# Moving 32 of 384 tokens out of the first expert matmuls of a PEER layer, and reordering filler work, dots and gates

## The chip, the cores and the metric

The kernel runs on one core of a Trainium2 chip. The metric is the time of one execution on the device in microseconds. The kernel before takes 1738.43 us, the median of three runs (1738.17 to 1740.97). The engines are TensorE (PE, with its weight loads as PEld), VectorE (DVE), ScalarE (ACT), GpSimd (POOL) and SyncE (SP, which only issues DMAs here). Each runs its own instructions in order; semaphores tie them together.

## The reference

One transformer layer on 512 tokens of 1024 float32 values.

- Token mixer: one projection `x @ w_in` gives the inputs of four attention branches, four heads of 64 each (top-128 selected keys; a window of 128 with sinks; block attention; stick-breaking), and four gates of 1024 columns. `merged = sum(sigmoid(g) * (y_branch @ w_branch))`, then `merged @ w_out`, a residual and a layer norm.
- PEER feed-forward: `q = x @ wq`; for each token and each of 8 heads two sets of 128 scores, the top 16 of each, the top 16 of their sums: 128 experts per token of 16384, with softmax gates. Then

```
h   = gelu(dot(x[token], u[expert]))      # 128 experts per token
out = sum over experts of gate * h * v[expert]
```

and a residual and a second layer norm.

## The kernel before, in words

Float32 products are made of three matmuls on halves: each operand is split into a high part (`w_hi`, `tok_hi`, written by ACT as a rounded copy) and a low part (`w_lo`, `tok_lo`, the difference, written by POOL or DVE), and `three` (line 1282) adds hi x hi, hi x lo and lo x hi. Weights come as units of 128 x 1024 values, loaded by SP into one of four `raw` slots (`load_unit`, line 337), split by ACT (`split_hi`, L535) and by POOL (`split_lo`, L435, `expert_lo`, L482) or DVE (`value_lo`, L1054). The counters `hi_done`, `lo_pool`, `lo_dve` and `unit_done` tie these steps; `raw`, `w_hi` and `w_lo` slots come free in the same order.

The order of the work is written out by hand, the same on every engine:

1. Attention. The first 9 of 38 units, then 32 items (`N_ITEM`), each one pair of heads on one tile of 128 queries. In step s PE does `scores(s + 1)`, `weights(s)`, `outputs(s - 1)` and then one whole projection unit as filler (`unit_at`: none in steps 16, 20 and 31). DVE does the softmax work of the item and `choose_keys` (`CHOICES[s]` rounds of top-8 removal for the key selection). The first unit waits for the low part of x, pair of chunks by pair of chunks.
2. Merge. For each of 8 column chunks four `branch` matmul groups, into four banks; DVE multiplies each with its gate (`prod`, L959) and adds (L962 to L966). `branch(c, b)` waits on `merge_step` for the first add of an earlier chunk.
3. Output projection, first norm, transposes of the new token tiles (`transpose_h`), their high and low parts (`hT_high` on ACT, `hT_low` on DVE), the query projection and the sub-key scores.
4. Experts, the dense way for tiles 1 to 3 (384 tokens, `DT`): for each of 128 units PE computes the activations of 128 experts for all 384 tokens (`project` at L1284 to L1286, 24 matmuls), ACT applies gelu (L703) and stores it to DRAM (`gelu_d`). Beside this, DVE routes one tile after the other (`route`: top-k, positions, gates), and in a marking stretch the gates of the tile are spread to a dense 128 x 128 table per token: `mark` builds one-hot rows for four tokens (a quad), ACT or DVE scales one side (L719, L1182), PE multiplies them (`gates_of`, L1571), ACT collects them in `stage` (L728) and stores 8 quads at a time to `gate_d` (L735). 14 units per routing stretch, 16 units with 2 quads each per marking stretch, 22 units in the tail (`TAIL`).
5. Tile 0 goes another way: POOL fetches for each of its 128 tokens the row `u[expert]` by an indirect DMA (`get_u`, L491), one fetch for all 128 partitions, into one of five slots, and DVE takes the dot with x (`dot`, L1060, x lies in PSUM banks 6 and 7). 128 dots; 30 per marking stretch, 3 or 6 per routing stretch, the rest in the tail. Later POOL fetches `v[expert]` (`get_v`, L499) and DVE adds it up with weight gate x gelu (`fma`, L1072), 128 of them between value units 2 and 116.
6. Value units: for each of 128 units DVE multiplies the stored gates (`gate_in`) with the stored activations (`gelu_in`) (`times_gelu`, L1195), ACT and DVE split the product, and PE does 18 matmuls of 512 columns (L1472 to L1475). SP loads the gates of the first 16 units in two parts (L373) at the weight loads P-8 and P-4 of the expert units, the rest later.
7. Second norm and stores.

What the diff and the steps of the prediction touch: `FIRST_UNITS`, `ROUTE_UNITS`, `MARK_UNITS`, `dots_by` (lines 65 to 93), `unit_at` (137), `load_gates` (365), `get_u` (485), `scale_match` (712), `store_gates` (733), `norm` (973), `dot` (1057), `route` (1075), `mark` (1170), `project` (1288), `branch` (1399), `last_units` (1478) and the loops that call them.

Of the kernel before, what the change touches and what calls it, by code (L numbers as in the profile page):

```python
# [24 lines left out]
P = 128  # L25
# [39 lines left out]
FIRST_UNITS, ROUTE_UNITS, MARK_UNITS = 16, 14, 16  # L65
TAIL = FIRST_UNITS + 3 * (ROUTE_UNITS + MARK_UNITS)
ROUTE_DOTS, MARK_DOTS = (3, 6, 6), 30
U_SLOTS, V_SLOTS = 5, 6
FMA_START, FMA_END = 2, P - 12
# [4 lines left out]
def routed_at(j):  # L74

    return FIRST_UNITS + (j - 1) * (ROUTE_UNITS + MARK_UNITS)


def dots_before(b):

    return sum(ROUTE_DOTS[:b]) + MARK_DOTS * b


def dots_by(k):

    if k < FIRST_UNITS:
        return 0
    b, at = divmod(k - FIRST_UNITS, ROUTE_UNITS + MARK_UNITS)
    if k >= TAIL:
        return min(P, dots_before(3) + (P - dots_before(3)) * (k - TAIL + 1) // (P - TAIL - 4))  # L90
    if at < ROUTE_UNITS:
        return dots_before(b) + ROUTE_DOTS[b] * max(0, at - 6) // (ROUTE_UNITS - 7)
    return dots_before(b) + ROUTE_DOTS[b] + MARK_DOTS * (at - ROUTE_UNITS + 1) // MARK_UNITS
# [38 lines left out]
CHOICES = [3] * 8 + [1] * 8 + [3, 2, 2, 2, 2, 3, 2]  # L132
# [4 lines left out]
def unit_at(s):  # L137

    n = N_FIRST + s - (s > 16) - (s > 20)
    return None if s in (16, 20) or n >= N_ATT or s < 0 else n  # L140
# [27 lines left out]
def peer_block(nc, xT, x_rows, w_units, u_units, v_rows, u_rows, sinks, ln1_g, ln1_b, subk, ln2_g, ln2_b,  # L168
# [98 lines left out]
    def sem(name):  # L267
# [17 lines left out]
    y_hi_set, y_lo_set, sig_kept, branch_full, merge_step, m_set = (sem(n) for n in (  # L285
        "y_hi_set", "y_lo_set", "sig_kept", "branch_full", "merge_step", "m_set"))
# [14 lines left out]
        "eid_set", "dot_done", "own_gelu", "fma_done", "own_x"))  # L301
    u_in = [sem(f"u_in{i}") for i in range(U_SLOTS)]
# [6 lines left out]
    def wait_lo(engine, n):  # L309
# [22 lines left out]
    with nc.Block() as block:  # L332
# [3 lines left out]
        def _(sp):  # L336
# [45 lines left out]
            def load_gelu(m):  # L382
# [5 lines left out]
                sp.dma_start(gelu_in[m % 2][:], gelu_d[:, first:first + GELU_GROUP, :])\  # L388
# [1280 lines left out]
```

## Time and profile before

| | before |
|---|---|
| median of 3 runs | 1738.43 us |
| the profiled execution | 1741.16 us |
| its span, first to last instruction | 1739.4 us |
| granted clock of TensorE, mean | 0.988 |
| PE, PEld busy | 1694.2, 1494.3 us |
| DVE, POOL, ACT busy | 1241.9, 822.3, 770.5 us |
| DMA moved | 417.65 MB, mean 240 GB/s |

Busy times are of the whole span and say nothing of a stage; the span falls into attention (to 341 us), merge and output projection (to 516), norm, queries and sub-keys (to 590), experts (to 1206) and values. A matmul's row shows when it starts and a modelled length of 0.3 to 0.4 us that overlaps with the next one's, so the pace is read from the distances of starts. An idle time stands with what ended it.

### The profile page before, as it was taken

The numbers are of one execution on the slowest core, as the hardware profiler recorded it, in microseconds if no ns is written. First come the engines' busy times: TensorE is split into PE (matmuls) and PEld (weight loads), VectorE is DVE, ScalarE is ACT, GpSimd is POOL, SyncE is SP. The second block draws the span as 40 slices with busy tenths as digits, with TensorE's granted clock in tenths as the row PEclk, the third lists the DMA queues.
The fourth block names the chain that finished last, engine by engine and source line by source line (L and its number), as shares of the span: only waits on it lengthen the run. The fifth ranks groups of instructions, "written<-read, shape, count | busy, mean of one in ns | idle before, by whom it ended". The sixth has DMA issues, their size and how long they took to land.

```text
span 1739.4 us, 24569 instructions
## 1 busy us (share of the span) xinstructions
PE 1694.2 (97%) x9061; PEld 1494.3 (86%) x9061; DVE 1241.9 (71%) x2490; ACT 770.5 (44%) x1301; POOL 822.3 (47%) x496
## 2 busy tenths in 40 slices
PE   7899979989999999999999999999999999999997
PEld 6678857778888999999999999999888888888886
DVE  2587884453244679588888988634888888888886
ACT  4444434532223443675477367534333333333332
POOL 5232222344446367776766686786423322323312
PEclk9999989999999999999999999999999999999999
DMA  5111111224233256899799789998999999999952
GB/s 199 62 61 62 49 49 61 73 85 145 71 123 109 93 182 204 280 387 359 235 333 378 259 286 384 373 369 293 406 391 354 389 370 351 379 378 353 387 193 85
DMA packets 126359, 417.65 MB, mean 240 GB/s; under 512 B 12960, under 2 KB 32416, under 8 KB 124704
## 3 DMA queue, kind: packets, MB, share of 16 engines
q1 hardware_dynamic: 70176, 232.81, 38.1%
q0 software_dynamic: 36864, 134.23, 20.5%
q10 hardware_dynamic: 19200, 49.03, 7.2%
q8 instruction: 73, 1.20, 0.3%
q14 instruction: 46, 0.38, 0.1%
HBM read 364.91 MB, written 50.86 MB: 239 GB/s over the span
## 4 chain that ended last, share of the span: by engine, by line
PE 94%; DVE 4%; DMA 1%; ACT 1%; issue 0%; POOL 0%; ACTq 0%; SPq 0%; DVEq 0%
PE ps L1284 18%; PE ps L1285 17%; PE ps L1286 17%; PE ps L1473 11%; PE ps L1475 11%; PE ps L1472 11%; PE ps L1571 5%; PE ps L1368 1%; PE ps L1393 1%; PE ps L1376 1%; PE ps L1347 1%; DVE dist_a L839 0%; DVE small L838 0%; DVE row L892 0%; DMA u_got<-u_rows,eid 0%
## 5 line engine op out<-in xcount | busy, mean ns | idle before, releaser
L1284 PE MATMUL ps<-tok_hi,w_hi 128*128 128x384 f32 (+2 forms) x1552 | 554.6, 357 | 13.4 <-DVE tok_lo L809 9.5
L1285 PE MATMUL ps<-tok_lo,w_hi 128*128 128x384 f32 (+2 forms) x1552 | 545.7, 352 | 0.0
L1286 PE MATMUL ps<-tok_hi,w_lo 128*128 128x384 f32 (+2 forms) x1552 | 545.3, 351 | 0.0
L535 ACT ACTIVATE w_hi<-raw 128x1024 fp32r<-128x1024 f32 x334 | 353.2, 1058 | 412.6 <-PE ps L1475 297.4
L482 POOL TENSOR_TENSOR w_lo<-raw,w_hi 128x1024 fp32r<-128x1024 f32 x128 | 319.3, 2497 | 164.7 <-ACT w_hi L535 164.2
L435 POOL TENSOR_TENSOR w_lo<-raw,w_hi 128x1024 fp32r<-128x1024 f32 x80 | 194.2, 2432 | 340.5 <-ACT w_hi L535 340.3
L1284 PEld LDWEIGHTS ps<-tok_hi,w_hi 128*128 128x128 f32 x1552 | 295.4, 190 | 39.1 <-issue 14.9
L1286 PEld LDWEIGHTS ps<-tok_hi,w_lo 128*128 128x128 f32 x1552 | 295.0, 190 | 19.5
L1285 PEld LDWEIGHTS ps<-tok_lo,w_hi 128*128 128x128 f32 x1552 | 295.5, 190 | 17.8
L1472 PE MATMUL ps<-w_hi,gh_hi 128*128 128x512 f32 x768 | 298.8, 389 | 0.0
L1473 PE MATMUL ps<-w_lo,gh_hi 128*128 128x512 f32 x768 | 298.8, 389 | 0.0
L499 POOL DMA_INDIRECT v_got<-v_rows,eid x128 | 151.4, 1183 | 302.6 <-DVE own L1072 285.4
L1475 PE MATMUL ps<-w_hi,gh_lo 128*128 128x512 f32 x768 | 236.4, 389 | 0.0
L1060 DVE CUSTOM_DVE_ANT_0 u_got<-u_got,ps 128x1024 f32<-128x1024 f32 x128 | 153.5, 1218 | 89.9 <-DMA u_got<-u_rows,eid 89.6
L1054 DVE TENSOR_TENSOR w_lo<-raw,w_hi 128x1024 fp32r<-128x1024 f32 x126 | 156.4, 1241 | 74.9 <-ACT w_hi L535 74.9
L1472 PEld LDWEIGHTS ps<-w_hi,gh_hi 128*128 128x128 f32 x768 | 144.2, 188 | 30.0
L1475 PEld LDWEIGHTS ps<-w_hi,gh_lo 128*128 128x128 f32 x768 | 144.1, 188 | 29.9
L1473 PEld LDWEIGHTS ps<-w_lo,gh_hi 128*128 128x128 f32 x768 | 144.1, 188 | 29.9
L1072 DVE SCALAR_TENSOR_TENSOR own<-v_got,w_own,own 128x1024 f32<-128x1024 f32 x126 | 159.9, 1278 | 0.0
L491 POOL DMA_INDIRECT u_got<-u_rows,eid x128 | 123.4, 964 | 27.2 <-issue 18.7
L703 ACT ACTIVATE gelu_t<-ps 128x384 f32<-128x384 f32 x120 | 58.8, 490 | 174.1 <-PE ps L1286 157.6
L1571 PE MATMUL ps<-right,left 128*128 128x128 f32 x768 | 93.5, 275 | 0.5 <-ACT right L719 0.5
(202 smaller groups left out, 1841.4 us busy)
## 6 DMA issues: line engine op xcount, KB each, us to landing
raw<-u_units SPq DMA_DIRECT2D x128, 512.0 KB, 4.5
raw<-v_rows SPq DMA_DIRECT2D x128, 512.0 KB, 6.8
raw<-w_units SPq DMA_DIRECT2D x78, 512.0 KB, 3.5
gate_d<-stage ACTq DMA_DIRECT2D x12, 2048.0 KB, 11.9
gelu_d<-gelu_t ACTq DMA_DIRECT2D x120, 192.0 KB, 4.5
gelu_in<-gelu_d SPq DMA_DIRECT2D x30, 768.0 KB, 7.7
gate_in<-gate_d SPq DMA_DIRECT2D x28, 768.0 KB, 11.9
gate_in<-gate_d SPq DMA_DIRECT2D x2, 1536.0 KB, 17.5
```

The lines of the kernel that those rows point to most:

```text
L435: pool.tensor_tensor(w_lo[:, n % RAW, :], raw[:, n % RAW, :], w_hi[:, n % RAW, :].bitcast(F32), ALU.subtract).then_inc(lo_done, 1)
L482: pool.tensor_tensor(w_lo[:, n % RAW, :], raw[:, n % RAW, :], w_hi[:, n % RAW, :].bitcast(F32), ALU.subtract).then_inc(lo_pool, 1)
L535: act.activation(w_hi[:, n % RAW, :], raw[:, n % RAW, :], ACT.Copy).then_inc(hi_done, 1)
L1054: dve.tensor_tensor(w_lo[:, n % RAW, :], raw[:, n % RAW, :], w_hi[:, n % RAW, :].bitcast(F32), ALU.subtract).then_inc(lo_dve, 1)
L1072: dve.scalar_tensor_tensor(own[e % 2][:], v_got[e % V_SLOTS][:], w_own[:, e:e + 1], own[e % 2][:], ALU.mult, ALU.add).then_inc(fma_done, 1)
L1284: pe.matmul(out_, l_hi, r_hi, start=start, stop=False)
L1285: pe.matmul(out_, l_hi, r_lo, start=False, stop=False)
L1286: return pe.matmul(out_, l_lo, r_hi, start=False, stop=stop)
L1472: pe.matmul(o, l_hi[:, tile_], wh, start=start, stop=False)
L1473: pe.matmul(o, l_hi[:, tile_], wl, start=False, stop=False)
L1475: last = pe.matmul(o, l_lo[:, tile_], wh, start=False, stop=stop)
L1571: last = pe.matmul(ps[:, 2 + q % 3, t * P:(t + 1) * P], left[:, s, t, :], right[:, s, t, :], start=True, stop=True)
```

## The change

- Tokens 128 to 159 (`NEAR`, 32 tokens) leave the expert matmuls: `UT` = 352 columns instead of 384, for gelu and its store too. Their activations are made like those of tile 0, by fetched rows and dots: 32 partitions times 4 groups of 32 experts each, so 32 fetches and 32 dots. Their expert numbers and x are spread over the partitions by DMAs issued on ACT. The activations after gelu are gathered by four DMAs and multiplied into the near tokens' gates before these are spread; in `gelu_in` the near columns are set to 1.
- The near tokens' quads are marked last, behind tile 3: 24, 32 and 40 quads in marking stretches of 14, 18 and 22 units. FIRST_UNITS 14, ROUTE_UNITS 17; 9 units in the tail.
- 160 dots: 12, 13, 13 in the routing stretches, 28, 36, 44 in the marking stretches, 6 in the tail and 8 beside the first value units. Three slots for the first 12, then five. fmas run from value unit 10 to 118.
- SP waits for the last gates in front of the first value weights; the first gate load follows that wait, the second comes after two weight loads. Value tile 3 uses banks 0 and 1.
- Attention: filler goes in chunks of three matmuls (`fill_to`, `filled_by`): 4 before the first scores, 4 in step -1, then 7 of 8 chunks in every step; two rounds of `choose_keys` in each of the steps 16 to 23.
- The first unit starts with the high parts of x. `branch` waits for the product that frees its bank. `transpose_h(1)` comes one unit earlier, `hT_low(0)` before the second half of the third tile's norm, `split_hi(U_WQ)` before `hT_high(0)`.

```diff
+NEAR = TOK
+UT = DT - NEAR
+NEAR_GROUPS = P // NEAR
+DOTS = P + NEAR
+FIRST_UNITS, ROUTE_UNITS, MARK_UNITS = 14, 17, (14, 18, 22)
+TAIL = FIRST_UNITS + 3 * ROUTE_UNITS + sum(MARK_UNITS)
+ROUTE_DOTS, MARK_DOTS, TAIL_DOTS, LATE_DOTS = (12, 13, 13), (28, 36, 44), 6, 8
+NEAR_FROM, NEAR_END = 54, 54 + NEAR
+FMA_START, FMA_END = LATE_DOTS + 2, P - 10
...
+def filled_by(s):
+    return 4 if s < -1 else KC + (KC * N_FILL - KC) * (s + 1) // N_ITEM
...
             for j in range(P):
                 load_unit(U_EXP + j, u_units[j])
-                if j == P - 8:
-                    sp.wait_ge(gate_read, N_QUAD)
-                    for s in range(2):
-                        sp.wait_ge(stage_out[s], 16 * (NB // 2))
-                    load_gates(0, 0)
-                if j == P - 4:
-                    load_gates(0, 1)
+            sp.wait_ge(gate_read, N_QUAD)
+            for s in range(2):
+                sp.wait_ge(stage_out[s], 16 * (NB // 2))
+            load_gates(0, 0)
             for j in range(P):
                 load_unit(U_VAL + j, v_rows[:, (j - KEPT) % P, :])
+                if j == 1:
+                    load_gates(0, 1)
...
+            def get_u(d):
+                slot, use, before = DOT_SLOTS[d]
+                near, e = dot_row(d)
+                if before is not None:
+                    pool.wait_ge(dot_done, before + 1)
...
+                if near and e == 0:
+                    pool.wait_ge(near_eid_in, 16 * NEAR_GROUPS)
...
+            def spread_near_x():
+                act.wait_ge(pick_set, 3)
+                for g in range(NEAR_GROUPS):
+                    act.dma_start(near_x[NEAR * g:NEAR * g + NEAR, :], x_tok[0:NEAR, 1, :]).then_inc(near_x_in, 16)
+            def finish_near():
+                act.wait_ge(dot_done, NEAR_END)
+                act.activation(near_dot[:], near_dot[:], ACT.Gelu).then_inc(near_gelu, 1)
...
+            def dot(d):
+                slot, use, before = DOT_SLOTS[d]
+                near, e = dot_row(d)
+                if d == NEAR_FROM:
+                    dve.wait_ge(near_x_in, 16 * NEAR_GROUPS)
+                    take_x(near_x[:], d)
+                if d == NEAR_END:
+                    take_x(x_tok[:, 0, :], d)
...
+            def weigh_near():
+                dve.wait_ge(near_h_in, 16 * NEAR_GROUPS)
+                dve.tensor_tensor(near_gate[0:NEAR, :], near_gate[0:NEAR, :], near_h[0:NEAR, :], ALU.mult)\
+                    .then_inc(near_pick, 1)
...
-                tokens = slice(P, S) if n >= U_EXP else slice(0, S)
-                to = ps[:, bank, 0:DT] if n >= U_EXP else ps[:, bank, :]
+                tokens = slice(P + NEAR, S) if n >= U_EXP else slice(0, S)
+                to = ps[:, bank, 0:UT] if n >= U_EXP else ps[:, bank, :]
...
-                    pe.wait_ge(merge_step, 4 * c - (7 if c < NH else 3))
+                    pe.wait_ge(prod_set, 4 * (c - (2 if c < NH else 1)) + (2, 3, 1, 0).index(b) + 1)
...
+            def fill_to(count):
+                while filled[0] < count:
+                    k, c = divmod(filled[0], KC)
+                    n = N_FIRST + k
+                    if c == 0:
+                        att_ready(n)
+                        wait_lo(pe, n)
+                    cols = slice(c * P, (c + 1) * P)
+                    last = three(ps[:, n % 2, :], w_hi[:, n % RAW, cols], w_lo[:, n % RAW, cols],
+                                 tok_hi[:, c, :], tok_lo[:, c, :], c == 0, c == KC - 1)
+                    filled[0] += 1
```

## Rows read from the trace of the kernel before

**Rows 1.** The page, its first part: each engine's busy us, share, instructions.
```profile
PE 1694.2 (97%) x9061; PEld 1494.3 (86%) x9061; DVE 1241.9 (71%) x2490; ACT 770.5 (44%) x1301; POOL 822.3 (47%) x496
```

**Rows 2.** Windows: length, busy us by engine, clock, DMA share, GB/s.
```profile
70.00:340.00 270.00, 255.07 (x1448) 195.45 (x1449) 191.72 (x448) 121.68 (x243) 72.95 (x30) 0.96 0.18 58
340.00:515.00 175.00, 170.39 (x752) 140.05 (x751) 71.21 (x95) 47.91 (x53) 72.65 (x32) 0.98 0.32 109
515.00:560.00 45.00, 41.23 (x277) 38.81 (x276) 25.90 (x33) 15.92 (x20) 28.85 (x12) 0.92 0.25 82
...
1019.00:1114.00 95.00, 95.00 (x641) 95.00 (x640) 80.22 (x135) 69.74 (x160) 68.01 (x48) 1.00 0.95 356
```

**Rows 3.** Timeline and chain, PE: starts of matmuls and of quads (start, length).
```profile
639.75 0.33 PE L1284 MATMUL ps<-tok_hi,w_hi 128*128 128x384 f32 x1
...
659.85 0.33 PE L1286 MATMUL ps<-tok_hi,w_lo 128*128 128x384 f32 x1
...
548.02 0.28 PE L1284 MATMUL ps<-tok_hi,w_hi 128*128 128x256 f32 x1
...
552.10 0.28 PE L1285 MATMUL ps<-tok_lo,w_hi 128*128 128x256 f32 x1
...
727.77 1.78 PE ps L1571 x16
733.72 1.78 PE ps L1571 x16
```

**Rows 4.** Timeline of the start.
```profile
7.00 6.24 DVE L809 TENSOR_TENSOR tok_lo<-x_raw,tok_hi 128x1024 fp32r<-128x1024 f32 x4 [7.00 <-ACT tok_hi L603]
...
9.48 0.77 PE L1284 MATMUL ps<-tok_hi,w_hi 128*128 128x512 f32 x1 [9.48 <-DVE tok_lo L809]
```

**Rows 5.** Windows of 8 us in the attention stage: an early item, a hole.
```profile
132.00:140.00 8.00, 7.73 (x49) 6.17 (x48) 7.05 (x16) 3.73 (x7) 2.40 (x1) 1.00 0.29 88
...
220.00:228.00 8.00, 3.23 (x12) 2.32 (x13) 7.66 (x22) 3.20 (x13) 0.00 (x0) 0.73 0.00 0
```

**Rows 6.** Timeline of the merge and of the first norm.
```profile
355.79 2.48 DVE L959 TENSOR_TENSOR prod<-ps,gates 128x512 f32<-128x512 f32 x4
...
359.14 0.76 PE L1284 MATMUL ps<-y_hi,w_hi 128*128 128x512 f32 x1 [4.37 <-DVE prod L962]
...
522.44 2.34 DVE L1006 TENSOR_TENSOR tok_lo<-ps,tok_hi 128x1024 fp32r<-128x1024 f32 x2
```

**Rows 7.** Waits: who waited for whom, us in total, times, longest.
```profile
DVE g_sum L1156 <- ACT pick L740: 20.9, 4, 10.4
...
DVE g_T L1168 <- PE ps L1560: 15.8, 3, 5.3
```

**Rows 8.** Groups of instructions by form, with count, busy us and mean ns.
```profile
L1060 DVE CUSTOM_DVE_ANT_0 u_got<-u_got,ps 128x1024 f32<-128x1024 f32 x128 | 153.5, 1218 | 89.9 <-DMA u_got<-u_rows,eid 89.6
```

**Rows 9.** A saturated window; the row fetches of the third marking stretch.
```profile
1236.00:1242.00 6.00, 6.00 (x28) 4.95 (x27) 6.00 (x9) 2.00 (x3) 4.70 (x3) 1.00 1.03 410
...
L491 POOL DMA_INDIRECT u_got<-u_rows,eid x31: 937/950/956, 1020.1 to 1113.9; - x31
...
DMA to landing us min/median/max: 5.2/8.1/12.6
```

**Rows 10.** Lines of DMAs in the tail: last gate store, gate loads, weight loads.
```profile
L735 ACTq DMA_DIRECT2D gate_d<-stage x1: 327/327/327, 1120.5 to 1120.5; - x1
...
DMA to landing us min/median/max: 10.0/10.0/10.0
...
L373 SPq DMA_DIRECT2D gate_in<-gate_d x2: 430/444/459, 1149.2 to 1165.8; - x2
...
DMA to landing us min/median/max: 17.0/17.5/18.1
...
L341 SPq DMA_DIRECT2D raw<-u_units x8: 327/363/3445, 1148.8 to 1179.4; - x8
...
DMA to landing us min/median/max: 6.2/11.8/15.2
```

More of the change, by code:

```diff
@@ new lines, in first_quad, with tile_quad, quads_of, stretch_dots @@
+def first_quad(b):
+    return max(0, 32 * (b - 1) - NEAR // 4) if b < NT else N_QUAD
+def tile_quad(q):
+    r = q + NEAR // 4
+    return r // 32 + 1, r % 32
+def quads_of(b, k):
+    first, count = first_quad(b), first_quad(b + 1) - first_quad(b)
+    return range(first + count * k // MARK_UNITS[b - 1], first + count * (k + 1) // MARK_UNITS[b - 1])
+def stretch_dots():
+    by = [0] * FIRST_UNITS
+    for b in range(1, NT):
+        for units, dots in ((ROUTE_UNITS, ROUTE_DOTS[b - 1]), (MARK_UNITS[b - 1], MARK_DOTS[b - 1])):
+            by += [by[-1] + dots * (k + 1) // units for k in range(units)]
+    units = P - TAIL
+    return by + [by[-1] + TAIL_DOTS * (k + 1) // units for k in range(units)]
@@ new lines, with dot_row, dot_slots @@
+DOTS_BY = stretch_dots()
+def dot_row(d):
+    if NEAR_FROM <= d < NEAR_END:
+        return True, d - NEAR_FROM
+    return False, d if d < NEAR_FROM else d - NEAR
+def dot_slots():
+    early = ROUTE_DOTS[0]
+    slots = [d % 3 for d in range(early)] + [(d - early + 3) % U_SLOTS for d in range(early, DOTS)]
+    last, plan = {}, []
+    for d, slot in enumerate(slots):
+        use, before = last.get(slot, (0, None))
+        plan.append((slot, use + 1, before))
+        last[slot] = (use + 1, d)
+    return plan
@@ L505, in rows_to @@
             def rows_to(n):
-                while got[0] < min(n, P):
+                while got[0] < min(n, DOTS):
                     get_u(got[0])
@@ L1225, in dots_to @@
             def dots_to(n):
-                while dots[0] < min(n, P):
+                while dots[0] < min(n, DOTS):
                     dot(dots[0])
@@ L1464, in _, with add_tile @@
                     branch(c, b)
-            def add_tile(n, t, l_hi, l_lo, start, stop, column):
+            def add_tile(n, t, bank, l_hi, l_lo, start, stop, column):
                 s = n % RAW
                 tile_ = slice(column * P, (column + 1) * P)
-                h = [(ps[:, 2 * t + a, :], w_hi[:, s, a * S:a * S + S], w_lo[:, s, a * S:a * S + S]) for a in range(2)]
+                h = [(ps[:, bank + a, :], w_hi[:, s, a * S:a * S + S], w_lo[:, s, a * S:a * S + S]) for a in range(2)]
                 for o, wh, wl in h:
@@ L1560, in turn_picks @@
                     last = pe.transpose(ps[:, 5, k * P:(k + 1) * P], pick[:, k, :], ident[:])
+                if b == NT - 1:
+                    pe.wait_ge(near_pick, 1)
+                    for k in range(3):
+                        last = pe.matmul(ps[:, 5, 3 * P + k * NEAR:3 * P + (k + 1) * NEAR],
+                                         near_keys[:, k, :] if k < 2 else near_gate[:], ident[:, 0:NEAR],
+                                         start=True, stop=True)
                 last.then_inc(pickT_full, 1)
```

276 lines of the change are left out of this document (172 added, 104 removed).

## The prediction

> **What bounds the kernel now.** I read the busy shares first, then the stages by window, then PE's waits, then the stretches in which the granted clock is low. PE is busy 1694.2 of 1739.4 us [rows 1]; the other engines are covered nearly everywhere. What PE loses stands in few places: 9.5 us before its first matmul [rows 4]; 14.9 us idle in the attention items, 4.6 us in the merge, 3.8 us between the two projections around the first norm [rows 2]; and the last tile's norm. The three middle stages also show a mean granted clock under 1 (0.96, 0.98, 0.92 [rows 2]): it falls to the lower of its two levels (1.2 GHz) in and behind these idle stretches. The expert stage, 590 to 1206 us, has no such loss (95.0 of 95 us in the third marking stretch [rows 2]), so there only less PE work helps, and only as long as the load that replaces it stays hidden.
>
> **The units.** Each expert unit has 24 matmuls over 384 tokens, now 352. 117 of them start from 639.75 to 659.85 us, 0.1733 us apart; 35 of 256 columns from 548.02 to 552.10 us, 0.120 us apart, both at full clock [rows 3]. The line through both is (columns + 32)/2.4 ns, which gives 0.160 us for 352. The neighbours bound it by 0.120 and 0.1733, and 384 is by far the nearer, so I take the line. 128 units x 24 x 0.0133 = 41.0 us less. The quads of the gates stay 96: eight leave token tile 1 and come back, as near tokens, behind tile 3. The value matmuls don't change. A unit with its quads lasts 5.95 us [rows 3], of which two quads take 5.946 - 4.16 = 1.79, so 0.893 each.
>
> **What carries the 32 tokens: rows, dots, DMA.** 32 row fetches of 0.95 us on POOL and 32 dots of 1.22 us on DVE are added [rows 8, 9], some 30 and 39 us of engines that aren't the bound. In the marking stretches there are now 54 units for 96 quads and 108 dots, before 48 for 96 and 90. One unit then lasts 24 x 0.160 + 1.78 x 0.893 = 5.43 us (96 quads over 54 units are 1.78). DVE was busy 80.2/16 = 5.01 us a unit [rows 2]; 0.125 dots more and fewer marks leave it under 5.17. POOL goes from 4.25 to about 4.4. Both fit. DMA is tight. A unit moves 0.524 MB of weights, 2 x 0.524 of rows, 0.180 of gelu and 1.78/8 x 2.097 = 0.466 of gates: 2.22 MB in 5.43 us, 409 GB/s, where before 2.23 MB in 5.95 us asked for 375 (measured 356 [rows 2]). The largest steady rate I find is 410 GB/s, at a share of 1.03, while PE doesn't wait [rows 9]. So the stretches sit at the ceiling. Bounds: 0 (all hidden) and 5.95 us a unit, the demand already carried, 54 x 0.52 = 28 us. I take 6 us, nearer to zero, since in the saturated stretch of rows 9 PE is full.
>
> The Trainium skill ("DMA: Bandwidth & Descriptors", section "Where 436 GB/s comes from") says that for transfers between HBM and SBUF the HBM share of about 358 GB/s per core binds, the fabric's 435 otherwise. By that page a unit would take 2.22/0.358 = 6.2 us and the stretches 42 us more, an estimate from its figure that would eat the whole saving of the units. The trace disagrees: 410 GB/s stand in rows 9 on this single busy core.
>
> **Routing.** Its stretches get 17 units x 3.84 = 65.3 us instead of 14 x 4.16 = 58.2. DVE has 12 or 13 dots there instead of 3 or 6, +8.5 us. DVE waited 5.3 us for PE each time, and before that 20.9 us in all for ACT's exponential [rows 7], which now comes two units earlier. The cover holds, price 0; if rows come late in it, PE would wait a few us at each of three turns. The copies that keep tile 1's picks (keep_near) come behind the first turn's picks, in this slack.
>
> **Near waits.** x of the near tokens is copied by four DMAs issued on ACT at the first marking unit of tile 2, behind the picks of tile 2; DVE needs it at the second dot of that unit. Behind DVE's wait are the next marks, and behind these ACT's scaling and PE's quads. The landing takes some 5 us (the shortest of a row is 5.2 [rows 9]), the copy into PSUM about a dot's 1.2, and 5.43 + 3.84 = 9.3 us lie between the turn and the second unit's quads, in which DVE also has three quads and a dot or two: I take 2.5 us, with the nine small matmuls and ACT's longer queue; bounds 0 and 5.
>
> **Entry to the value units.** The tail has 9 units instead of 22, 34.6 us. SP now waits for the last gates and their store in front of the first value weights and of the gate loads; everything on SP's queue stands behind it. The last store goes out 6 us into the tail and lands 10 us later [rows 10]. Then two loads of 1.57 MB and the value weights start together at 16 to 19 us. A gate load took 17.0 and 18.1 us [rows 10], so the second lands at 34 to 37, and gh of unit 0 needs 3 us more. PE arrives at 34.6. I expect 3 us of waiting, between 0 and 10 (the upper with PE's clock down after it). Late dots (8) and fmas packed into 108 instead of 114 units stay under DVE's time: price 0.
>
> **Attention.** Filler units came whole, one per item, none at items 16, 20 and 31; now 7 of 8 chunks go with every item and 8 chunks before the second item's scores. There are three holes (at 72, 222 and 254 us); in 220 to 228 us PE is busy 3.2 of 8 us, clock 0.73 [rows 5]. Together they are the stage's 14.9 us idle and most of its lost clock, 0.04 x 270 = 10.8 us [rows 2]; part of that fell while PE was idle, so about 24 us are to be had, as all PE work stays. But DVE is busy 7.05 of 8 us in an ordinary early item [rows 5], and an item with 0.875 unit lasts only some 7.1 us, so part of the idle time comes back in small waits. Bounds 4 and 24, I take 15 us gain.
>
> **Start, merge, norm.** Unit 0 now starts on x's high parts: DVE's first low part begins at 7.00, when the high part is there, PE at 9.48 [rows 4]. Gain 2.2 us, between 0 and 2.5; then POOL's second low part, at 15.7 us, is what is late. In the merge PE waited 4.4 us for the adds of a chunk (359.14), though the product that frees its bank begins at 355.79 [rows 6]; now it waits for that product, 1.8 us. With the clock, gain 4, between 1 and 5.5. Around the norm PE waited 3.8 us for tok_lo, whose two parts ran together from 522.44 [rows 6]; the transpose goes one matmul group (1.4 us) earlier and the first part moves ahead. Gain 3.5, between 0 and 6.4; DVE's scaling stands between the two parts and can be late.
>
> **Sum**, against the profiled execution (1741.16 us, span 1739.4, 1.8 around it; 2.7 above the median 1738.43): -41.0 + 6 + 2.5 + 3 - 15 - 2.2 - 4 - 3.5 = -54.2 us. On the median: 1684 us.
>
> **Rivals.**
> (a) The row pipeline sets the marking. Five slots and two rows a unit: a row has to land and be consumed within two units. Rows take 8.1 us, up to 12.6 [rows 9], two units are 10.9. At 11.9 us a unit lasts 5.95: 1684 - 6 + 28 = 1706. For it: DVE waits for rows in these stretches already. Against it: DVE works ahead and PE has never waited.
> (b) The same, past the point of no gain: without the 6 us the sum is -60.2, over 54 units 1.11 us each, so 6.54 us a unit, a typical row of 13.1 us. At 15.2 us, the longest that a weight load took while gates were loaded [rows 10], it is 7.6 us a unit, +118: 1796, slower. Against it: 8.1 us is far off, and in the saturated window of rows 9 PE was busy 6 of 6 us.
> (c) Attention gains nothing: DVE is the bound and the holes spread out: 1699.
> (d) A 352-column matmul costs what 384 does: 1725.
>
> **Chances.** Forecast 0.68, (a) 0.13, (b) 0.04, (c) 0.12, (d) 0.03. About 0.2% (3.5 us) is what can be told from no change. Faster: all but (b) and a sliver, 0.94; same 0.02; slower 0.04. The own terms, all at their good ends, give -41 - 24 - 2.5 - 5.5 - 6.4 = -79; half way there is 1667. Upwards (a) with its neighbours reaches 1710. Range 1664 to 1712.
>
> **What would show it.** Matmuls of the expert units 0.160 us apart; the stretches of attention without windows of low clock; marking units 5.43 us apart (5.5 or more: DMA or rows); PE's wait at the first value matmul with gates landing; the landing times of rows, whose median I expect at 8 to 9.5. I am wrong if PE sits idle in the marking stretches by more than 10 us, or if the attention keeps its 15 us of idle time.

## The result, and the profile after

| | before | after |
|---|---|---|
| median us (7 runs each) | 1738.43 | 1754.59 |
| runs from .. to | 1737.52 .. 1742.12 | 1746.84 .. 1757.94 |
| profiled execution us | 1741.16 | 1754.68 |
| its span | 1739.4 | 1752.9 |
| granted clock, mean | 0.988 | 0.986 |

The ratio is 1.0078 [1.0058, 1.0098]: 0.8% slower, where I had forecast 1684 us, 3% faster. (Of the kernels below, e9 and e10 had one slow run each, 4517 and 2985 us, which the ratios leave out.) The page of after has PE with 23 us less work than in [rows 1] and DVE with 82 us more:

```profile
PE 1671.0 (95%) x9067; PEld 1464.7 (84%) x9067; DVE 1323.7 (76%) x2561; ACT 765.3 (44%) x1302; POOL 847.0 (48%) x530
```

So PE does less and the kernel lasts longer: PE waits. To see where, I cut both spans at two marks: the end of the scores of the subkeys, behind which ACT splits the next expert weight (590.52 us before, 579.95 after), and the first value matmul (1205.69 and 1211.23). These are windows of before (length, busy us of PE, PEld, DVE, ACT, POOL, clock, DMA share, GB/s):

```profile
0.00:590.50 590.50, 557.00 (x2936) 447.73 (x2937) 322.59 (x664) 231.81 (x385) 216.03 (x107) 0.97 0.26 86
590.50:1205.70 615.20, 614.74 (x3824) 614.32 (x3823) 475.07 (x1280) 346.24 (x655) 443.23 (x258) 1.00 0.84 303
1205.70:1739.00 533.30, 522.43 (x2305) 432.24 (x2304) 444.19 (x547) 192.49 (x262) 163.00 (x131) 0.99 0.90 337
```

The same three of after, and below them the entry of the value units and the rest of them:

```profile
0.00:580.00 580.00, 547.81 (x2937) 436.75 (x2938) 333.49 (x664) 230.25 (x386) 216.49 (x107) 1.00 0.26 88
580.00:1211.20 631.20, 597.14 (x3828) 593.31 (x3827) 531.92 (x1330) 341.29 (x656) 459.27 (x284) 0.98 0.87 315
1211.20:1752.00 540.80, 526.03 (x2304) 434.68 (x2304) 458.30 (x569) 193.74 (x264) 171.21 (x140) 0.99 0.90 336
...
1211.00:1250.00 39.00, 34.37 (x136) 27.82 (x137) 27.83 (x41) 13.58 (x19) 14.56 (x12) 0.91 0.94 354
1250.00:1720.00 470.00, 470.00 (x2075) 389.24 (x2075) 410.22 (x490) 172.57 (x235) 147.37 (x124) 1.00 0.95 352
```

So the part ahead of the experts is 10.6 us shorter, the expert stage 16.1 us longer though its matmuls are narrower, the value stage 8.0 us longer. In the expert stage PE was idle 0.5 us before and 34.1 us now. The waits say for whom (PE, after, 580 to 1260 us; us in total, times, longest):

```profile
PE ps L1742 <- DVE pick L1278: 18.7, 3, 8.2
PE ps L1429 <- POOL w_lo L541: 8.5, 3, 4.9
PE ps L1655 <- DVE gh_lo L1341: 6.7, 2, 4.4
PE ps L1759 <- ACT right L793: 4.5, 4, 3.5
```

L1742 is the turn of a tile's picks: PE now waits 8.2, 5.9 and 4.6 us for the end of each route. L1429 is an expert matmul that waits for the low part of its weights on POOL. Neither wait exists before. What POOL waits for in the same stage, 620 to 1215 us:

```profile
POOL u_got L555 <- DVE h_own L1175: 58.6, 25, 9.4
POOL w_lo L541 <- ACT w_hi L606: 53.2, 41, 5.9
...
POOL u_got L555 <- DVE near_dot L1175: 13.1, 11, 4.7
```

Before, POOL waited 2.3 us in all for dots and 135.5 us for ACT's high parts: it had time over. Now a row fetch on POOL waits for the dot that frees its slot, and the low parts queued behind the fetch wait with it. The timeline of after shows it twice, at the end of route 1 and in route 3 (the row at 691.72 is the fourth of the four low parts in the row above it):

```profile
683.54 0.95 POOL L555 DMA_INDIRECT u_got<-u_rows,eid  x1 [2.95 <-DVE h_own L1175]
684.33 9.45 DVE L1261 TENSOR_TENSOR ps<-c_col,iota 128x2048 f32<-128x2048 f32 x1
684.51 11.47 POOL L541 TENSOR_TENSOR w_lo<-raw,w_hi 128x1024 fp32r<-128x1024 f32 x4
...
691.72 4.26 POOL L541 TENSOR_TENSOR w_lo<-raw,w_hi 128x1024 fp32r<-128x1024 f32 x1
...
1027.51 0.95 POOL L555 DMA_INDIRECT u_got<-u_rows,eid  x1 [9.42 <-DVE h_own L1175]
1028.47 4.67 POOL L541 TENSOR_TENSOR w_lo<-raw,w_hi 128x1024 fp32r<-128x1024 f32 x2
```

The comparison that starts at 684.33 lasts 2.30 us where nothing holds it up and 9.45 here, beside four low parts back to back. 9.45 is 2.30 and three low parts of 2.4, and the fourth low part, which otherwise lasts 2.4, lasts 4.26: it waited for the comparison in turn. At 1027.51 the fetch had waited 9.4 us, the low part ran only then, and PE waited 4.9 us for it.

### The profile page after: what moved, and what is told of

Same layout as the page of the kernel before. It is cut to its first block, busy times and chain, and to the rows that moved or that the text cites. A ratio compares the mean times of both kernels' runs of the same rounds, so it can differ in the third digit from the quotient of the medians.

```text
span 1752.9 us, 24712 instructions
## 1 busy us (share of the span) xinstructions
PE 1671.0 (95%) x9067; PEld 1464.7 (84%) x9067; DVE 1323.7 (76%) x2561; ACT 765.3 (44%) x1302; POOL 847.0 (48%) x530
## 4 chain that ended last, share of the span: by engine, by line
PE 67%; DVE 20%; DMA 5%; issue 4%; ACT 2%; POOL 1%; ACTq 0%; SPq 0%; DVEq 0%; POOLq 0%
PE ps L1429 10%; PE ps L1655 10%; PE ps L1656 10%; PE ps L1658 10%; PE ps L1430 10%; PE ps L1431 10%; PE ps L1759 3%; DMA u_got<-u_rows,eid 3%; DVE u_got L1175 3%; DVE ps L1261 2%; DMA gelu_in<-gelu_d 1%; PE ps L1514 1%; DVE dist_a L943 1%; DVE row L996 1%; DVE ps L1265 1%
## 5 line engine op out<-in xcount | busy, mean ns | idle before, releaser
L1429 PE MATMUL ps<-tok_hi,w_hi 128*128 128x352 f32 (+2 forms) x1544 | 542.7, 351 | 20.4 <-POOL w_lo L541 8.5
L1430 PE MATMUL ps<-tok_lo,w_hi 128*128 128x352 f32 (+2 forms) x1544 | 532.0, 345 | 0.0
L1431 PE MATMUL ps<-tok_hi,w_lo 128*128 128x352 f32 (+2 forms) x1544 | 531.8, 344 | 0.0
L541 POOL TENSOR_TENSOR w_lo<-raw,w_hi 128x1024 fp32r<-128x1024 f32 x128 | 309.9, 2425 | 89.5 <-ACT w_hi L606 84.9
L494 POOL TENSOR_TENSOR w_lo<-raw,w_hi 128x1024 fp32r<-128x1024 f32 x80 | 194.7, 2437 | 326.5 <-ACT w_hi L606 326.3
L1429 PEld LDWEIGHTS ps<-tok_hi,w_hi 128*128 128x128 f32 x1544 | 293.9, 190 | 48.0 <-issue 21.6
L1175 DVE CUSTOM_DVE_ANT_0 u_got<-u_got,ps 128x1024 f32<-128x1024 f32 x160 | 190.7, 1216 | 57.4 <-DMA u_got<-u_rows,eid 42.1
L773 ACT ACTIVATE gelu_t<-ps 128x352 f32<-128x352 f32 x120 | 55.3, 461 | 160.0 <-PE ps L1431 146.3
```

Of the source, the lines that this page charges most:

```text
L494: pool.tensor_tensor(w_lo[:, n % RAW, :], raw[:, n % RAW, :], w_hi[:, n % RAW, :].bitcast(F32), ALU.subtract).then_inc(lo_done, 1)
L541: pool.tensor_tensor(w_lo[:, n % RAW, :], raw[:, n % RAW, :], w_hi[:, n % RAW, :].bitcast(F32), ALU.subtract).then_inc(lo_pool, 1)
L1175: dve.tensor_tensor_reduce(out=u_got[slot][:], in0=u_got[slot][:], in1=ps[:, 6:8, :].rearrange("p a n -> p (a n)"), scale=1.0, scalar=0.0, ...
L1429: pe.matmul(out_, l_hi, r_hi, start=start, stop=False)
L1430: pe.matmul(out_, l_hi, r_lo, start=False, stop=False)
L1431: return pe.matmul(out_, l_lo, r_hi, start=False, stop=stop)
```

## The experiments

Medians; each ratio is to the kernel before on the same chip, where that had 1738.4 to 1740.6 us. Where a kernel is set against after or against another experiment below, it is by the difference of the ratios, times 1738. e3 and e8 leave out part of the computation, e4 too, of which there is one run and no ratio. Routes 1 to 3 are timed from a route's first maximum to the start of its last operation, in the timeline of the one profiled run; a turn is the point at which PE needs a route's picks, and the column has PE's waits there.

| kernel | us | ratio | routes | turns |
|---|---|---|---|---|
| before | 1738.4 | 1 | 62.2, 54.5, 56.0 | none |
| after | 1754.6 | 1.0078 [1.0058, 1.0098] | 77.1, 75.2, 75.2 | 8.2, 5.9, 4.6 |
| e1 front only | 1731.5 | 0.9953 [0.9941, 0.9966] | | |
| e2 experts only | 1758.4 | 1.0117 [1.0102, 1.0132] | | 18.9 in all |
| e3 narrow units | 1718.3 | 0.9887 [0.9869, 0.9905] | 56.8, 56.3, 55.4 | 0, 1.7, 1.7 |
| e5 dots out | 1730.6 | 0.9950 [0.9937, 0.9963] | 57.1, 56.0, 57.9 | none |
| e6 the same, 15 units | 1731.1 | 0.9955 [0.9941, 0.9968] | 51.9, 55.3, 60.4 | 0, 1.2, 4.5 |
| e7 iota in PSUM | 1734.7 | 0.9975 [0.9967, 0.9984] | 72.6, 71.6, 71.9 | 0.9, 0.4, 0.5 |
| e8 no near rows | 1715.2 | 0.9867 [0.9851, 0.9882] | 77.1, 63.6, 65.2 | 8.2, 0, 0 |
| e9 e6, gates early | 1727.3 | 0.9929 [0.9914, 0.9944] | 51.9, 56.6, 59.8 | 0, 0.7, 2.1 |
| e10 e9, iota, near | 1725.8 | 0.9916 [0.9901, 0.9931] | 52.8, 56.1, 62.3 | 0, 0.7, 4.7 |
| e11 e10, 8 dots to the tail | 1727.9 | 0.9935 [0.9917, 0.9952] | 52.8, 55.7, 55.9 | none |
| e12 near dots later | 1746.2 | 1.0038 [1.0020, 1.0055] | 77.1, 74.7, 76.6 | 8.2, 6.3, 4.7 |

**e1 and e2: the two halves of the change.** Each takes one half of the diff: e1 the attention's fillers, `first_unit`, `prod_set` and the order around the norm, e2 everything else.

> The kernel before with only the part of the change that lies ahead of the experts (filler chunks in the attention items, first unit on x's high parts, merge waiting for the products, order of transposes and tile splits around the norm). My theory since the result: this part is a gain, the expert and value stages are the loss. In the profile after, the experts start at 579.95 us instead of 590.52, so I expect 10.6 us less than before, 1728 us, ratio 0.994. Rival: it only shifts stalls that the old expert stage would show again; then no difference.

> The kernel after with the part ahead of the experts as it was before (whole filler units, old start, merge and norm). By the milestones the expert stage is 16.1 and the value stage 8.0 us longer than before, so I expect 24 us more than before, 1762 us, ratio 1.014. Rival: the loss comes from the two parts meeting (the earlier start of the experts finds other state); then under 1750.

The front alone gains 0.5%, the experts alone lose 1.2%; the two together (+0.7%) are the whole change (+0.8%) within the intervals. Both sizes (8 and 20 us) came out 2 to 4 us under what I read from the marks.

**e3: only the narrower units.** Tokens 128 to 159 get no expert activations at all.

```diff
-tokens = slice(P, S) if n >= U_EXP else slice(0, S)
-to = ps[:, bank, 0:DT] if n >= U_EXP else ps[:, bank, :]
+tokens = slice(P + 32, S) if n >= U_EXP else slice(0, S)
+to = ps[:, bank, 32:DT] if n >= U_EXP else ps[:, bank, :]
```

> The kernel before with the expert matmuls over 352 instead of 384 tokens and nothing else: tokens 128 to 159 are left out of the expert activations (their output is not computed rightly). It gives what the narrower units are worth alone. By the pace read in the profile after (0.158 or 0.167 us a matmul, 0.1733 for 384): 128 x 24 x 0.0103 = 31 us less, 1707. By my forecast (0.160): 41 less, 1697. Rival: the other engines were the bound behind PE already, the turns of the routing stretches (14 units x 3.9 = 55 us for a route that needs about 53) or the marking (DVE, DMA at 2.33 MB per 5.7 us = 409 GB/s) give waits on PE; then less than 20 us gained.

20 us, 27 in the profiled spans: my 41 us were never there. PE's waits in this kernel are 7 us in all, from 580 to 1260 us:

```profile
PE ps L1560 <- DVE pick L1159: 3.5, 2, 1.7
PE ps L1571 <- ACT right L719: 2.0, 2, 1.5
PE ps L1284 <- ACT gelu_t L703: 1.9, 1, 1.9
```

Of the 14 us that the profiled span stays short of 41, these waits are 7, and the pace is about 8, which is all of it: the expert matmuls of this kernel start 0.1627 us apart on average, not 0.160, over 3072 of them. Why the medians are only 20 us apart, where these two executions are 27, wasn't traced. What each width costs is what e4 measures.

**e4: eight widths.**

```diff
+WIDTHS = (384, 376, 368, 360, 352, 344, 336, 320)
-tokens = slice(P, S) if n >= U_EXP else slice(0, S)
+width = WIDTHS[(n - U_EXP) // 4 % len(WIDTHS)] if n >= U_EXP else S
+tokens = slice(S - width, S)
```

> The kernel before with expert matmuls of 384, 376, 368, 360, 352, 344, 336, 320 columns, four units each, in turn (the columns left out are not computed). Read from the trace: time from one matmul start to the next. If the line (columns + 32)/2.4 ns holds: 0.1733, 0.170, 0.1667, 0.1633, 0.160, 0.1567, 0.1533, 0.1467 us. If widths that aren't a multiple of something cost more or have two paces, it is 352 and its neighbours that leave the line, with 0.158 or 0.167 for 352.

The first matmul of each block of four units (96 matmuls of one width, at full clock, without a wait between them):

```profile
601.78 0.33 PE L1285 MATMUL ps<-tok_hi,w_hi 128*128 128x376 f32 x1
...
618.42 0.33 PE L1285 MATMUL ps<-tok_hi,w_hi 128*128 128x368 f32 x1
...
634.42 0.33 PE L1285 MATMUL ps<-tok_hi,w_hi 128*128 128x360 f32 x1
...
650.42 0.32 PE L1285 MATMUL ps<-tok_hi,w_hi 128*128 128x352 f32 x1
...
665.62 0.32 PE L1285 MATMUL ps<-tok_hi,w_hi 128*128 128x344 f32 x1
...
680.99 0.32 PE L1285 MATMUL ps<-tok_hi,w_hi 128*128 128x336 f32 x1
```

The differences over 96 give 0.1733 us for 376 columns, 0.1667 for 368 and for 360, 0.1583 for 352 and 0.1601 for 344: stairs, not a line, and 344 dearer than 352. But 360 and 352 have two paces each. The block of 360 columns that starts at 957.91 us runs at 0.1633 behind its first dozen, the line's value. In after 352 runs at one and at the other (96 matmuls in the first pair, 90 in the second):

```profile
639.90 0.32 PE L1431 MATMUL ps<-tok_hi,w_lo 128*128 128x352 f32 x1
...
655.10 0.32 PE L1431 MATMUL ps<-tok_hi,w_lo 128*128 128x352 f32 x1
...
799.74 0.33 PE L1431 MATMUL ps<-tok_hi,w_lo 128*128 128x352 f32 x1
...
814.74 0.33 PE L1431 MATMUL ps<-tok_hi,w_lo 128*128 128x352 f32 x1
```

15.20/96 = 0.1583 us and 15.00/90 = 0.1667. In after the pace is 0.1583 up to PE's wait at the first turn (701.66 us), 0.1667 up to one at 966.01, but for a few us around 868 and 879, 0.1583 up to one at 1096.87 and 0.1667 to the end; so the changes lie at or near waits of PE. 384 columns in before show one pace only. What sets it wasn't found.

**e5: the dots out of the routing stretches.** All of the change's work is done, 23 dots stand elsewhere.

```diff
-ROUTE_DOTS, MARK_DOTS, TAIL_DOTS, LATE_DOTS = (12, 13, 13), (28, 36, 44), 6, 8
-NEAR_FROM, NEAR_END = 54, 54 + NEAR
+ROUTE_DOTS, MARK_DOTS, TAIL_DOTS, LATE_DOTS = (3, 6, 6), (30, 36, 44), 20, 15
+NEAR_FROM, NEAR_END = 41, 41 + NEAR
```

> The kernel after with 23 of the 38 dots moved out of the three routing stretches, into the tail and the value units: ROUTE_DOTS (3, 6, 6) as before instead of (12, 13, 13), marking (30, 36, 44), tail 20, late 15, near dots 41 to 72. All work of the change stays. My theory: the loss of the expert stage is the routing stretches. With 12 or 13 dots POOL waits for dots before it can fetch rows, its low parts pile up and run back to back, DVE's operations on SBUF wait behind them, and PE waits at the turns (8.2 + 5.9 + 4.6 us) and for w_lo (2.9 + 4.9), with some 8 us of lower clock. Then this kernel is 25 to 30 us below the kernel after: about 1727. Rival A: the marking stretches (DMA, rows) or the near rows are what costs; these carry as much or more here, so under 10 us gained, 1745 or more. Rival B: the value stage can't take 15 late dots; then PE waits in the value units.

22 us below after, a little less than expected. Route 1 has 9 dots less and is 20.0 us shorter, though it now holds a wait of 5.2 us for ACT's exponential. In after its 12 dots took 14.3 us and 7.9 us of waiting for rows, and the one comparison 9.45 us; these are its groups (624.1 to 701.5 us):

```profile
L1175 DVE CUSTOM_DVE_ANT_0 u_got<-u_got,ps 128x1024 f32<-128x1024 f32 x12 | 14.3, 1219 | 7.9 <-DMA u_got<-u_rows,eid 7.7
L1261 DVE TENSOR_TENSOR ps<-c_col,iota 128x2048 f32<-128x2048 f32 x1 | 9.5, 9452 | 0.0
```

The same two groups in e5 (623.3 to 680.8 us):

```profile
L1175 DVE CUSTOM_DVE_ANT_0 u_got<-u_got,ps 128x1024 f32<-128x1024 f32 x3 | 3.7, 1220 | 0.1
...
L1261 DVE TENSOR_TENSOR ps<-c_col,iota 128x2048 f32<-128x2048 f32 x1 | 2.8, 2832 | 0.0
```

And POOL's low parts come one by one, each after ACT's high part:

```profile
664.34 2.39 POOL L541 TENSOR_TENSOR w_lo<-raw,w_hi 128x1024 fp32r<-128x1024 f32 x1 [0.72 <-ACT w_hi L606]
668.14 3.00 POOL L541 TENSOR_TENSOR w_lo<-raw,w_hi 128x1024 fp32r<-128x1024 f32 x1 [1.41 <-ACT w_hi L606]
```

Rival A falls as the whole story: the marking carries the same rows and dots, and the waits for turns and for low parts are gone. What is left in e5 stands at the value units (8.5 us), at the last expert units (6.9 us) and in the marking, where PE waits 8.4 us for scaled matches instead of 4.5. POOL still waits 64 us for dots in this stage, but PE doesn't wait for what stands behind.

**e6: a longer tail.** e5 with `ROUTE_UNITS` 15 instead of 17.

> The previous kernel with 15 instead of 17 units in each routing stretch, so that the tail behind the last gates has 15 units instead of 9. Theory: a route with 6 dots lasts some 57 us, 15 units of 3.9 us are 58, so no new wait at the turns; and gates and gelu land before the value units start (2.3 + 4.4 us of waiting gone, and some clock), 5 us below the previous kernel: 1722. Rival: the two units were cover that the route needs; then waits of 2 to 4 us at each turn, and it is slower than the previous one.

No gain: a wait of 4.5 us at the third turn, and at the first value matmul 9.5 us, where e5 has 8.5. The rival was right for the third turn; the first doesn't wait and the second 1.2 us. SP issued the gate loads at 1161.40 and 1169.63, behind all expert loads, though PE began the last quads at 1122.61. Whether that is why the entry didn't improve is what e9 tries.

**e7: one input of two comparisons in PSUM.** No dot, row or unit moves.

```diff
-hot = ps[:, 2:6, :].rearrange("p a (k c) -> p (a k) c", c=EK)
+hot = ps[:, 2:4, :].rearrange("p a (k c) -> p (a k) c", c=EK)
+settled(dve.tensor_copy(ps[:, 4, 0:EK], iota[:, 0:EK]))
...
-settled(dve.tensor_tensor(hot, rank[:].unsqueeze(2).to_broadcast([P, EH * EK, EK]),
-                          iota[:, 0:EK].unsqueeze(1).to_broadcast([P, EH * EK, EK]), ALU.is_equal))
+for i in range(2):
+    settled(dve.tensor_tensor(hot, rank[:, part].unsqueeze(2).to_broadcast([P, half, EK]),
+                              ps[:, 4, 0:EK].unsqueeze(1).to_broadcast([P, half, EK]), ALU.is_equal))
```

> The kernel after with one input of the route's two comparisons (c_row or c_col against iota) read from PSUM instead of SBUF; for that the table is built in two halves. No dot, unit or row is moved. In the profile after these comparisons take 6.6 us instead of 2.7, four times. Port theory: they are slow because both inputs lie in SBUF and GpSimd is at work; with one in PSUM they take their 2.3 us, the route is 8 us shorter, and most of the waits at the three turns (18.7 us) goes: 1733 to 1738. Rival: it is the number of dots and the wait for their rows that makes the route long; the time only moves to the next operation: 1750 or more.

18 us below after, from eight comparisons. The second comparison of a route, from 780 to 860 us, first in e7 and then in after:

```profile
L1265 DVE TENSOR_TENSOR ps<-c_col,ps 128x1024 f32<-128x1024 f32 x2 | 2.5, 1226 | 0.0
```

```profile
L1261 DVE TENSOR_TENSOR ps<-c_col,iota 128x2048 f32<-128x2048 f32 x1 | 7.0, 7031 | 0.0
```

Each route is some 4 us shorter, route 0 of the own tokens too (it ends at 620.0 instead of 624.0), and the turns' 18.7 us shrink to 1.8. PE's waits for scaled matches grow from 4.5 to 9.0 us. The waits for low parts stay (8.9 us), as they should: POOL still waits for dots. So that both inputs lie in SBUF is shown as one link; that the waits for low parts go with the dots (e5) and not with the comparison makes the order on POOL's queue another.

The Trainium skill ("SBUF — State Buffer", section "SBUF: two separate sides") says that DVE and GpSimd share a port pair as an exclusive lock, that a DVE operation with two SBUF inputs takes it against a GpSimd operation that reads SBUF, and that who starts first holds it for the whole instruction. The trace agrees on who is hit. On the rest it shows something else: the profile has the comparison starting 0.18 us ahead of the first low part (684.33 and 684.51), and yet it waited, and not for one low part but for three (9.45 us).

**e8: no near rows.** 32 fetches, 32 dots and their copies are left out, and with them the near tokens' activations. The marking stretches have 18, 26 and 32 dots, the routing stretches keep 12, 13 and 13.

> The kernel after without the near rows: their 32 row fetches, 32 dots and the copies of near eid and x are left out (the near tokens' activations are wrong), the marking stretches have (18, 26, 32) dots instead of (28, 36, 44), the routing stretches keep (12, 13, 13). My theory (the routing stretches cost) expects the waits at the turns to stay: 5 to 10 us below the kernel after (the wait for near_x and what follows it, 6 us, goes): 1747. Rival A (the added rows and their DMA in the marking): 20 to 25 us below, 1732.

37 us below after, half as much again as even the rival gave. My single cause was too narrow. Turn 1 waits 8.2 us as in after, since nothing is changed ahead of it; turns 2 and 3 don't wait, with the same 13 dots. The difference is how DVE comes into them. In e8 DVE waits for PE in the marking, 29.2 us in all, where in after that row is missing:

```profile
DVE u_got L1175 <- DMA u_got<-u_rows,eid: 41.0, 18, 4.3
DVE left L1315 <- PE ps L1759: 29.2, 25, 2.5
```

Route 2 starts at 770.8 us in e8, 5.1 us before PE starts the last quads of the marking; in after at 782.8, 2.8 us behind that start. In the marking ahead of it DVE worked 55.0 us and waited 2.0 us for rows in e8, against 66.3 and 14.2 in after. And POOL waits 12.4 us for dots instead of 71.7, so its low parts come one by one in route 2. That is what makes the route shorter, 63.6 us for 75.2 with 13 dots in both and no wait for rows in either: DVE's other operations take 48.6 us instead of 60.1. The comparison of e7 is one of those held up, and small ones are too. The first rows are of after, where the fetch had waited for the dot just ahead, the last is the same operation in e8:

```profile
806.71 5.08 DVE L1218 TENSOR_TENSOR cand<-s_top 128x128 f32<-128x128 f32 x1
806.89 4.74 POOL L541 TENSOR_TENSOR w_lo<-raw,w_hi 128x1024 fp32r<-128x1024 f32 x2
...
794.76 0.29 DVE L1218 TENSOR_TENSOR cand<-s_top 128x128 f32<-128x128 f32 x1
```

So for turns 2 and 3 it takes both: many dots in the route, and a DVE and a POOL that come to it without a lead (a lead is work done ahead of what PE needs). Few dots without a lead cost nothing at turns (e5), many dots with one nearly nothing (e8). Turn 1 fits, as route 1 follows route 0 at once and has no lead in either kernel, but it also has three slots only, and a route 1 with more wasn't run. e8 lightens DVE, POOL and the DMA together, so which of them gives the lead isn't separated.

**e12: x of the near tokens in time.** `NEAR_FROM` 58 instead of 54, nothing else.

> The kernel after with the near dots at 58 to 89 instead of 54 to 85, nothing else: four own dots come between the turn and the first near dot, so that x of the near tokens has landed by then. In the profile after DVE waits 6.3 us for it, and PE 3.5 us behind that at 873.94. My forecast priced this wait at 2.5 us; then 2 to 4 us below the kernel after. If DVE's lateness is what makes the third route long (rows not fetched ahead, low parts in a pile), the third turn's wait of 4.6 us and the w_lo wait of 4.9 us shrink too: 8 to 12 us below, 1744. Rival: it is DVE's and POOL's whole load in the routing stretches alone; then within 2 us.

7 us below after, between my two cases (2 to 4 and 8 to 12), and each of the two kernels is known to 3 or 4 us. And not where I said: the third turn's wait is 4.7 as before. What went is DVE's 6.3 us for near_x, PE's 3.5 us behind it, 2 us of waits for low parts and clock.

**e9 to e11: towards a version that beats both.** e9 is e6 with the first gate loads where before has them; the loads behind all expert loads, not shown here, go:

```diff
 for j in range(P):
     load_unit(U_EXP + j, u_units[j])
+    if j == P - 8:
+        sp.wait_ge(gate_read, N_QUAD)
+        for s in range(2):
+            sp.wait_ge(stage_out[s], 16 * (NB // 2))
+        load_gates(0, 0)
+    if j == P - 4:
+        load_gates(0, 1)
```

> The kernel of the 15-unit routes (dots out of the routing stretches, tail of 15 units) with the first gate loads back at the loads of units P-8 and P-4, as before the change, instead of behind all expert loads. There PE waited 9.5 us at the first value matmul while the last gates had left PE 70 us earlier: the loads were issued only at 1161 and 1170 us. My theory: the entry wait is their late issue on SP's queue, and it goes: 1731 - 9 = 1722. Rival: it is the DMA, full of rows and weights in the tail, that delays their landing; then issuing them earlier delays the rows and the time stays within 3 us.

4.5 us below e6, half of what was expected and not far clear of the intervals. SP's timeline of e9 has the loads 25 us earlier than in e6:

```profile
1136.30 0.38 SPq L433 DMA_DIRECT2D gate_in<-gate_d  x1
...
1142.66 0.59 SPq L433 DMA_DIRECT2D gate_in<-gate_d  x1
```

The 9.5 us at the first value matmul are gone, and a new wait has taken part of them (PE, e9, 580 to 1260 us, the two largest):

```profile
PE ps L1430 <- ACT gelu_t L774: 6.4, 1, 6.4
PE ps L1760 <- ACT right L794: 6.1, 8, 1.5
```

At 1153.01 PE waits 6.4 us for ACT's gelu of a unit two before. ACT does that gelu at 1152.51, behind a high part that waited for its weights:

```profile
1151.55 1.06 ACT L607 ACTIVATE w_hi<-raw 128x1024 fp32r<-128x1024 f32 x1 [11.41 <-DMA raw<-u_units]
```

So an expert weight landed late. That the two gate loads issued at 1136.30 and 1142.66, which move beside it, delay it is likely and not shown; the rival, the DMA, would then be half right.

e10 adds the comparison of e7 and `NEAR_FROM` 43; e11 moves 8 more dots into the tail (`(28, 34, 40), 28, 15`, `NEAR_FROM` 39).

> The same with the comparisons of the route reading iota from PSUM and the near dots beginning four dots behind the turn instead of two, so that x of the near tokens can land. Theory: the route gets 2 us shorter each (waits of 1.2 and 4.5 us at the turns go) and DVE's 3 to 5 us for near_x go: 6 us below the kernel without these two, 1716, under both kernels and under the first part alone. Rival: these waits are covered by what PE does anyway; within 2 us of the kernel without.

> The previous one with 8 dots moved from the marking stretches into the tail: (28, 34, 40) instead of (30, 36, 44), tail 28, near dots right behind the turn (39). In the marking PE waits several times about 1 us for the scaled matches, behind DVE's dots and their rows. Theory: some of these 8 us and of the clock go, 3 to 5 us below the previous one. Rival: the tail (28 rows in 15 units beside the gate loads) becomes the place where rows or gates are late; 2 to 6 us above.

Neither can be told from e9, where I expected 6 us for the one and 3 to 5 more for the other. In e10 the third route is longer again (62.3 us). In e11 the waits at the turns are gone, those for scaled matches in the marking hardly less (5.0 us, 5.8 in e10), and the tail has taken their place: 7.2 us for gelu, again behind a late expert weight (13.3 us), and 6.2 us at the first value matmul, the rival's case. e9, e10 and e11 beat before by 0.7 to 0.8%, after by 25 to 28 us. e10 beats e1 as well (0.9916 against 0.9953, intervals apart); for e9 and e11 the intervals touch. e9, e10 and e11 are the fastest of the kernels here that compute everything.

## Why the prediction was wrong, step by step

Measured by the span, the forecast was -54.2 us and the measured difference +13.5: 67.7 us to account for. The marks are PE's first matmul on y_hi (336.42 before, 325.58 after), the first on m_hi (475.6, 466.1) and the two of above.

| step | forecast | measured | off |
|---|---|---|---|
| start and attention | -17.2 | -10.8 | 6.4 |
| merge | -4 | +1.3 | 5.3 |
| norm | -3.5 | -1.1 | 2.4 |
| units, marking, routing, near waits | -32.5 | +16.1 | 48.6 |
| entry and value units | +3 | +8.0 | 5.0 |

**Routing, "The cover holds, price 0": the step that failed.** The cover didn't hold: PE waited 18.7 us at the three turns and 8.5 us for low parts. Three things were wrong in the step. I counted the dots at their 1.22 us [rows 8] and nothing for the rows they wait for, which the same row had as 89.9 us over 128 dots, 0.7 us each. (This showed in route 1 alone, 7.9 us; in routes 2 and 3 DVE waited 0.2 us for rows. And +8.5 us is for seven more dots; route 1 has nine more, 11 us.) I counted on DVE's slack of 5.3 us for PE and 20.9 for ACT's exponential [rows 7]; both are used up in after (3.2 us are left of the first). And I looked only at DVE: what the dots do to POOL's queue, on which fetches and low parts stand in one order, and what POOL's low parts in a burst do to DVE, was in no sum. This third thing was the large one: in route 2 DVE's operations other than dots take 11.5 us more than in e8. That the same comparison (L1142) lasts 2.3 us as a rule in before and up to 4.4 was there to be read. The fallback I wrote, "PE would wait a few us at each of three turns", was the right place with a chance too small to be named among the rivals.

How the 48.6 us divide: at the forecast pace the 127 units behind the mark save 40.6 us, and the stage got 16.1 longer, so 56.7 us have to be found (8.5 of them I had allowed for, in the marking and the near waits). The real paces save some 9 less. PE is idle 34.1 us where it was 0.5. The rest, about 14 us, I put down to PE being busy at a lower clock behind these waits: by the windows the lost clock is some 11 us, part of it while PE was idle, so a few us stay open. The windows of the second and the third routing and marking show the clock (700 to 860, 860 to 1045 us):

```profile
700.00:860.00 160.00, 149.62 (x943) 148.83 (x944) 143.40 (x359) 83.86 (x161) 116.66 (x76) 0.97 0.87 315
860.00:1045.00 185.00, 170.82 (x1096) 169.33 (x1095) 163.63 (x387) 102.58 (x203) 131.45 (x84) 0.97 0.89 321
```

**Units.** The line through 256 and 384 columns [rows 3] was drawn through a stair. e3 shows what the units are worth, waits included: 20 us instead of 41, of which the pace explains 8.

**Marking, +6.** A little too high: between the turns and the ends of the three marking stretches PE is idle 4.6 us, 3.5 of them behind near_x. What I said of DMA was right in the main. The longest window of after stands at a share of 1.00, and PE loses nearly nothing in it, where [rows 2] had 0.95 and 356 GB/s; the rate is 381 GB/s, not my 409, as the units ran at the slower pace:

```profile
1060.00:1160.00 100.00, 99.34 (x684) 98.37 (x683) 82.79 (x139) 71.87 (x164) 75.99 (x54) 1.00 1.00 381
```

So rivals (a) and (b) were wrong too: rows that land late were no bound on PE in the marking. They were one on DVE, 14.2 us in the first marking against 2.0 in e8, which lost its lead by them and by its added work (e8), and it was paid in the next route. I had the right quantity, the latency of rows, and looked for its price in the wrong stretch.

**Near waits, +2.5.** 7 us by e12, give or take 5. DVE's wait was 6.3 us; that it costs more than PE's own wait behind it (3.5) I had not counted.

**Entry, +3.** PE waits 2.25 us at the first value matmul, as forecast. The second wait, 4.4 us at 1246.10 for a gelu load that took 20.3 us to land beside two gate loads, was not in the sum, nor the mean clock of 0.91 in the window with them (1211 to 1250 us).

**Attention, -15.** The holes did go, and the clock in the stage is 1.00 where it was 0.96 [rows 2]: at 260 us of length about 10 us. The idle time stayed: 248.00 of 258 us busy, 10 us idle against 14.9. PE now waits 0.2 to 1.2 us for row in 11 places, which is what I had named as the limit (DVE busy 7.05 of 8 us [rows 5]); I priced it too low. The stage gained 8.4 us without the start, so rival (c), nothing, was about as near as the forecast, 15.

**Merge.** The wait for the sums is 2.3 instead of 4.4 us [rows 6], but another of 4.2 us stands behind it, at a unit of the gates:

```profile
345.77 0.47 PE L1429 MATMUL ps<-y_hi,w_hi 128*128 128x512 f32 x1 [2.34 <-DVE prod L1063]
...
355.68 0.77 PE L1429 MATMUL ps<-tok_hi,w_hi 128*128 128x512 f32 x1 [4.22 <-issue]
```

The trace gives no releaser for it, but the kernel does: ahead of the first two late units of the gates PE waits for the first add of the third chunk. That add lasts 0.69 us in e1, and 2.24 here, beside a low part on POOL that starts at 352.69:

```profile
353.34 2.24 DVE L1065 TENSOR_TENSOR prod<-prod,prod 128x512 f32<-128x512 f32 x1
```

It ends 0.10 us before PE starts, in e1 too, where PE's wait is 1.2 us. I had freed `branch` from the adds and left this wait on one.

**A slip in the range.** Half way from 1684 us to the good end (-79, 1659 us) is 1671 or 1672, not 1667. The measured time lies above the range, so this end of it doesn't matter here.

**What was right:** the start (first matmul at 7.04 us instead of 9.48), that DMA carries the marking, PE's wait at the first value matmul, and that DVE's and POOL's totals fit. The totals were true and decided nothing.

## What to carry to other kernels

An engine with 25% idle time (DVE here, busy 76%) can still be late: ask at each hand-over what lead it has, and who spends it one stretch later. When work is added to a queue that also carries something the bound engine needs, price the wait at the head of that queue, not only the work; and look at both directions of a shared port. An interpolated duration of an instruction is two measurements and a guess.

## What the runs showed of the hardware that I had not expected

- The time of a matmul is a stair in its columns: 376 as 384 (0.1733 us), 360 as 368 (0.1667), 344 at 0.1601, 336 at 0.1533, 320 at 0.1467 (e4). 352 runs at 0.1583 or at 0.1667 (after) and changes between them, often at a wait, and stays at the slower one while the granted clock is 1.00: 26 us over 128 units between the best and the worst. 360 has two paces as well (0.1667, 0.1633).
- A DVE operation with two inputs in SBUF waited for three GpSimd operations in a row (9.45 us for 2.30, after), a small one for two (5.08 for 0.29, after and e8); with one input in PSUM the comparison waited for none in 16 of them (1.223 to 1.230 us each, e7).
